# Norm factors in a PSUM bank, a root one step sooner, and two sums finished ahead of a branch, in a two-block kernel

## What is computed

```python
def dsa_attention(q, k, v, q_idx, k_idx, w_idx, rel_bias):
    ...
        p = jax.nn.softmax(logits, axis=-1).astype(v.dtype)
        return jnp.einsum('bqhk,bqkhd->bqhd', p, v_sel)

def hgrn2(q, f_pre, i, g_out, lb, norm_g):
    lb = lb.reshape(B_HEADS, B_HEAD_DIM).astype(jnp.float32)
    f = lb + (1.0 - lb) * jax.nn.sigmoid(f_pre.astype(jnp.float32))
    log_f = jnp.log(f)
    kk = 1.0 - f
    ...
    o = jnp.transpose(o, (1, 0, 3, 2, 4)).reshape(bsz, seq, B_HEADS, B_HEAD_DIM)
    o = rmsnorm_2(o, norm_g) * jax.nn.silu(g_out.astype(jnp.float32))

def hier_moe(h, rg_w, rg_b, re_w, re_b, w_gate, w_up, w_down):
    ...
    for gi in range(N_GROUPS):
        hg = jax.nn.silu(jnp.einsum('nd,edf->nef', x, wg[gi])) * jnp.einsum('nd,edf->nef', x, wu[gi])
        y = y + jnp.einsum('nef,efd->nd', hg * gates[:, gi, :, None], wd[gi])

def second_block(...):
    lb_soft = jax.nn.softmax(hgrn_lb_raw.astype(jnp.float32), axis=0)
    lb_all = jnp.cumsum(lb_soft, axis=0) - lb_soft[0:1]
    ...
    return rmsnorm_2(x, final_norm_g)
```

## Time and profile before

| | us |
|---|---|
| runs, median (lowest to highest) | 2004.6 (2003.86 to 2004.92) |
| the profiled execution, its own time | 2007.65 |
| its span, first to last instruction | 2005.9 |
| PE busy in the span | 1664.8 |
| DVE busy | 985.1 |
| ACT busy | 551.2 |
| POOL busy | 610.1 |
| mean granted clock of PE | 0.936 |

### The profile page before, as it was taken

The page is one execution under the profiler, slowest core; times in us unless marked ns, Lnnn a source line. Parts: engine busy times, 40 slices in busy tenths (PEclk is TensorE's granted clock), DMA queues, the critical chain, the costliest instruction groups (busy, mean ns, idle before and its releaser), DMA issues.

```text
span 2005.9 us, 22036 instructions
## 1 busy us (share of the span) xinstructions
PE 1664.8 (83%) x8692; PEld 1026.3 (51%) x8692; DVE 985.1 (49%) x1895; ACT 551.2 (27%) x959; POOL 610.1 (30%) x396
## 2 busy tenths in 40 slices
PE   7899986777777777778999998999999967677765
PEld 7785842232222223237989988987895311111211
DVE  6462766876778775553573896554434100000001
ACT  4342421212212212114443545445621000000001
POOL 3331633444445444435563205433320000000000
PEclk9999988999999999999999999999999877778778
DMA  8755599999999999995544433544588999999997
GB/s 336 303 196 218 204 366 413 421 421 421 422 421 422 421 421 418 421 380 171 168 147 141 144 126 126 185 168 147 178 349 309 421 421 421 422 421 421 422 421 306
DMA packets 92373, 634.88 MB, mean 317 GB/s; under 512 B 10956, under 2 KB 13772, under 8 KB 16616
## 3 DMA queue, kind: packets, MB, share of 16 engines
q1 hardware_dynamic: 50832, 353.39, 45.2%
q0 software_dynamic: 36864, 268.45, 32.5%
q10 hardware_dynamic: 4568, 11.56, 1.6%
HBM read 632.28 MB, written 1.08 MB: 316 GB/s over the span
## 4 chain that ended last, share of the span: by engine, by line
PE 44%; DMA 39%; DVE 11%; ACT 3%; issue 2%; POOL 0%; ACTq 0%; SPq 0%; DVEq 0%; POOLq 0%
DMA t<-in_expert_uv,t 19%; DMA t<-in_ed 7%; DMA t<-in_eg 6%; PE ps L589 5%; PE ps L594 5%; PE ps L591 5%; DMA ring<-in_ed 4%; PE ps L819 3%; PE ps L653 3%; DVE t L2106 3%; PE ps L822 3%; DMA ring<-in_eg 3%; PE ps L666 3%; PE ps L609 2%; PE ps L610 2%; PE ps L615 2%
## 5 line engine op out<-in xcount | busy, mean ns | idle before, releaser
L181 POOL TENSOR_TENSOR t<-ring,t 128x1024 fp32r<-128x1024 f32 x125 | 315.9, 2540 | 486.8 <-ACT t L173 486.6
L819 PE MATMUL ps<-t 128*128 128x512 f32 x488 | 268.6, 633 | 158.3 <-ACT t L1469 158.1
L2778 POOL DMA_INDIRECT t<-in_expert_uv,t x244 | 275.7, 1130 | 354.8 <-PE ps L822 334.1
L2106 DVE CUSTOM_DVE_ANT_0 t<-t 128x1024 f32<-128x1024 f32 x244 | 299.8, 1234 | 164.4 <-DMA t<-in_expert_uv,t 161.8
L173 ACT ACTIVATE t<-ring 128x1024 fp32r<-128x1024 f32 x220 | 230.1, 1054 | 227.8 <-PE ps L594 77.8
L822 PE MATMUL ps<-t 128*128 128x512 f32 x488 | 254.6, 604 | 0.0
L819 PEld LDWEIGHTS ps<-t 128*128 128x128 f32 x488 | 85.1, 193 | 317.1 <-ACT t L1469 254.5
L1125 PE MATMUL ps<-t 128*32 128x512 f32 x856 | 142.3, 763 | 70.2 <-DMA t<-in_eg 27.7
L181 DVE TENSOR_TENSOR t<-ring,t 128x1024 fp32r<-128x1024 f32 x95 | 131.9, 1395 | 135.0 <-ACT t L173 134.4
L589 PE MATMUL ps<-t 128*128 128x256 f32 x1120 | 165.0, 291 | 12.6 <-ACT t L173 6.6
L1462 ACT ACTIVATE t<-t 128x2 f32<-128x2 f32 x129 | 26.2, 203 | 507.4 <-DVE t L2106 507.0
(11 more groups left out here) (383 smaller groups left out, 1915.4 us busy)
## 6 DMA issues: line engine op xcount, KB each, us to landing
ring<-in_w_in SPq DMA_DIRECT2D x82, 1024.0 KB, 5.0
t<-in_eg SPq DMA_DIRECT2D x43, 1024.0 KB, 26.7
t<-in_ed SPq DMA_DIRECT2D x36, 1024.0 KB, 27.1
t<-in_eu SPq DMA_DIRECT2D x28, 1024.0 KB, 27.0
ring<-in_eu SPq DMA_DIRECT2D x27, 1024.0 KB, 26.4
ring<-in_ed SPq DMA_DIRECT2D x21, 1024.0 KB, 27.0
ring<-in_ada_w SPq DMA_DIRECT2D x20, 1024.0 KB, 7.6
ring<-in_eg SPq DMA_DIRECT2D x17, 1024.0 KB, 27.7
```

What stands on the lines that cost most here:

```text
L181: e.tensor_tensor(p.lo, p.view, p.hi.bitcast(F32), ALU.subtract).then_inc(self.w.lo[eng], 1)
L819: ins = e.matmul(sums[tt][0], s.diag[col % 4], v[:, 1024:1536], start=first, stop=last)
L2106: ins = e.tensor_tensor_reduce(out=g[:, 0:1024], in0=g[:, 0:1024], in1=s.hN[:, col // 128, :], scale=1.0, scalar=0.0, op0=ALU.mult, op1=AL ...
L2778: m.gathered[s.place[col]].up(e.indirect_dma_start(out=s.gb[col], out_offset=None, in_=m.a_in["expert_uv"], in_offset=bass.IndirectOffsetO ...
```

## The change

It has six edits.

- `dve_attention`: the four bound operations stand behind the output subtractions.
- `pe_recurrence`: the bank that would be claimed next is taken out of the ring during the stage, and its first 80 columns are `h.stat`. `dve_recurrence` keeps the sums and the inverse roots there (indices 0 and 3); mean squares, roots and the polishing's temporary stay in SBUF.
- `act_recurrence`: `pour(filler, 2)` for `pour(filler, 4)` ahead of the root.
- `dve_inv_sqrt`, with more than one column: one operation fewer and two fused ones.
- `act_squares`: the first halves are squared ahead of the branch on ACT, the second halves behind it.
- `dve_experts`: the first halves are multiplied with the norm's row ahead of the last result `y(7, 1)`; behind the branch the second halves of both tiles are made by one fused operation each. Both engines' dense paths repeat the early work.

```diff
@@ pe_recurrence
+    whole, kept = list(b.usable), b.usable[b.next % 8]
+    b.usable, b.next = [i for i in b.usable if i != kept], b.next % 8
+    h.stat, h.stat_free = b.ps[kept][:, 0:80], (b.out[kept], b.uses[kept])
...
     pe_turn(m, e, "obT", r3(h.bq, 2), 8, m.h_out)
+    b.usable, b.next = whole, whole.index(kept)
@@ act_recurrence
-    pour(filler, 4)
+    pour(filler, 2)
@@ new, and called ahead of the branch with n = 0 and behind it with n = 1
+def act_squares(m, e, n):
+    o, b = m.s4, m.b
+    junk = o.xg[1].rearrange("p a b -> p (a b)")[:, 0:512]
+    for tt in range(2):
+        e.wait_ge(*b.full(("sum4", tt, n)))
+        ins = e.activation(junk, b.ap(("sum4", tt, n)), ACT.Square, accum_out=o.fin[:, 2 * n + tt:2 * n + tt + 1])
+        if tt == 0:
+            m.a(ins)
+        else:
+            m.norm_sum.up(ins)
+    e.wait_ge(m.norm_sum.sem, m.norm_sum.n)
@@ dve_inv_sqrt
     else:
-        m.v(e.tensor_tensor(t, r, r, ALU.mult))
-        m.v(e.tensor_tensor(t, t, ms, ALU.mult))
-    m.v(e.tensor_scalar(t, t, -0.5, 1.5, ALU.mult, ALU.add))
-    m.v(e.tensor_tensor(r, r, t, ALU.mult))
+        m.v(e.scalar_tensor_tensor(out=t, in0=ms, scalar=-0.5, in1=r, op0=ALU.mult, op1=ALU.mult))
+        m.v(e.tensor_tensor(t, t, r, ALU.mult))
+        m.v(e.scalar_tensor_tensor(out=r, in0=t, scalar=1.5, in1=r, op0=ALU.add, op1=ALU.mult))
@@ dve_recurrence
-    h_ss, h_ms, h_sq, h_r, h_t = (h.sst[:, 16 * i:16 * i + 16] for i in range(5))
+    h_ss, h_ms, h_sq, h_r, h_t = ((h.stat, h.sst)[i in (1, 2, 4)][:, 16 * i:16 * i + 16] for i in range(5))
+    e.wait_ge(*h.stat_free)
@@ dve_experts, ahead of the wait for ("y", q, n)
+            if q == 7 and n:
+                e.wait_ge(m.d_row0.sem, 48)
+                e.wait_ge(*m.norm_sum.turn("dve"))
+                for tt in range(2):
+                    ins = e.tensor_tensor(o.ys[:, tt, :], b.ap(("sum4", tt, 0)), m.grow[0][:, 0:512], ALU.mult)
+                m.v(ins)
@@ vector_program, behind the branch: the same two removed here, and
-    e.wait_ge(*m.norm_sum.turn("dve"))
-    m.v(e.tensor_tensor(hold[:, 0, 512:1024], b.ap(("sum4", 0, 1)), m.grow[0][:, 512:1024], ALU.mult))
...
-    m.fin_row.up(e.tensor_scalar(hold[:, 0, 512:1024], hold[:, 0, 512:1024], f[:, 8:9], None, ALU.mult))
-    m.fin_row.up(e.scalar_tensor_tensor(out=hold[:, 1, 512:1024], in0=b.ap(("sum4", 1, 1)), scalar=f[:, 9:10],
-                                        in1=m.grow[0][:, 512:1024], op0=ALU.mult, op1=ALU.mult))
+    for tt in range(2):
+        m.fin_row.up(e.scalar_tensor_tensor(out=hold[:, tt, 512:1024], in0=b.ap(("sum4", tt, 1)), scalar=f[:, 8 + tt:9 + tt],
+                                            in1=m.grow[0][:, 512:1024], op0=ALU.mult, op1=ALU.mult))
```

More of the change, by code:

```diff
@@ L1785, in act_dense @@
     e.wait_ge(*b.full("sum5"))
+    for tt in range(2):
+        junk = o.xg[1].rearrange("p a b -> p (a b)")[:, tt * 512:tt * 512 + 512]
+        b.emptied(e.activation(junk, b.ap(("sum4", tt, 0)), ACT.Square, accum_out=o.fin[:, tt:tt + 1]), ("sum4", tt, 0))
+    for tt in range(2):
+        e.wait_ge(*b.taken(("sum4", tt, 0)))
+def act_squares(m, e, n):
[9 more added lines that the diff above has]
+    e.wait_ge(m.norm_sum.sem, m.norm_sum.n)
 def scalar_program(m, e):
@@ L1806, in scalar_program @@
     e.activation(m.st[:, 60:61], m.one, ACT.Sqrt)
-    for n in range(2):
-        for tt in range(2):
-            e.wait_ge(*b.full(("sum4", tt, n)))
-            ins = e.activation(o.xg[1].rearrange("p a b -> p (a b)")[:, 0:512], b.ap(("sum4", tt, n)), ACT.Square,
-                               accum_out=o.fin[:, 2 * n + tt:2 * n + tt + 1])
-            if n == 0 and tt == 0:
-                m.a(ins)
-            else:
-                m.norm_sum.up(ins)
-                e.wait_ge(m.norm_sum.sem, m.norm_sum.n)
+    act_squares(m, e, 1)
     e.wait_ge(*m.norm_ms.turn("act"))
@@ L2713, in dve_dense @@
     e.wait_ge(*b.full("sum5"))
+    for tt in range(2):
+        e.wait_ge(*b.taken(("sum4", tt, 0)))
+        m.v(e.tensor_tensor(o.ys[:, tt, :], b.ap(("sum4", tt, 0)), m.grow[0][:, 0:512], ALU.mult))
 def vector_program(m, e):
@@ L2735, in vector_program @@
     hold = r3(m.hold, 2)
-    e.wait_ge(m.d_row0.sem, 48)
-    e.wait_ge(*m.norm_sum.turn("dve"))
-    for tt in range(2):
-        ins = e.tensor_tensor(o.ys[:, tt, :], b.ap(("sum4", tt, 0)), m.grow[0][:, 0:512], ALU.mult)
-    m.v(ins)
-    e.wait_ge(*m.norm_sum.turn("dve"))
-    m.v(e.tensor_tensor(hold[:, 0, 512:1024], b.ap(("sum4", 0, 1)), m.grow[0][:, 512:1024], ALU.mult))
     e.wait_ge(*m.norm_sum.turn("dve"))
```

13 lines of the change are left out of this document (8 added, 5 removed).

## The result

The changed kernel took 1994.11 us (median of five runs, 1992.75 to 1996.77) against 2004.6 for the kernel before: ratio 0.9948, 95% interval 0.9937 to 0.9959. That is 10.5 us less, where 8.8 were forecast. A second series gave 1996.3 against 2004.34, ratio 0.9959 (0.9946 to 0.9973), 8.0 us less. The kernel before in that series ran from 2003.03 to 2008.54, so single runs scatter by several microseconds. A difference of one or two can be read only inside a trace, between two rows.

A forecast was written before the change was run, and what follows sets the result against it. Expert weight streaming fills the DMA engines, so only time saved on TensorE ahead of line 1107 or behind the last weight counts. 4.1 + 2.6 + 0.1 + 1.95 = 8.75 us, giving 1995.8 us; range 1992.8 to 2000.0.

The forecast's parts named there:

- Part 1: Attention's end: moving the four bound operations behind the attention output cuts TensorE's stall; gain 4.1 us, bounds 2.6 and 5.0.
- GpSimd got in first: Attention's end: GpSimd goes ahead of the first low half, leaving TensorE idle 0.87 us instead of 3.45.
- Part 2: Recurrence's norm: sooner root, factors partly in PSUM and one operation fewer bring the transposes together; gain 2.6 us.
- so I keep the slow clock in: Recurrence's norm: a 1.5 us gap stays, so the slow clock behind it is assumed to remain; otherwise gain 4.2.
- even if every operation stayed blocked, 1239.9: Recurrence's norm: with operations blocked as before, products still end at 1239.9, ahead of TensorE's transposes at 1241.69.
- The bank costs nothing: Level loop, seven banks: nearest claim has 2.3 us left, so no cost; slower rival, 2009.9 us, chance 0.04.
- Part 3: Shorter polishing at the end of retrieval, hidden in retention: one operation less; gain 0.1 us (0 to 0.2).
- Part 4: Kernel's end: early squares and products let the sum of squares start 2.05 us sooner; net gain 1.95 us.
- the 3 from which it would have counted: ScalarE's branch at the end: from 3 us each microsecond counts; at 5, time 1997.8; rival's chance 0.08.
- From line 1107 on all rows should be sooner by the same 6.8 us: Routing onward: sign that all rows, and the last weight too, come 6.8 us sooner.
- the 3.05 us between the profiled execution and the median: Whole kernel: the profiled execution lies 3.05 us above the runs' median, turning a 1997.1 span into 1995.8.

The follow-up runs named there:

- experiment 4: The kernel before with only the root of the recurrence's norm taken after two pours instead of four, no bank, old polishing; 2003.79 us, ratio 0.9997.
- experiment 3: The kernel before with the end's edits alone (first halves squared and scaled ahead of the branch), old polishing; 2003.49 us, ratio 0.9992.

## Why the prediction was right, point by point

The time forecast, 1995.8, lies between the two series (1994.11 and 1996.3), and the sum of 8.75 us between their gains. Term by term it was less exact, and that the total fits so well is in part luck.

| place, fourteen traces | values |
|---|---|
| attention, to line 923 | 21.26 to 21.30 (5 with the bounds ahead), 19.39 (two ahead), 17.07 to 17.10 (6 with all four behind), 16.07 and 16.08 (low half first) |
| norm gap | 6.0 to 6.6 (6 without the bank), 3.85 or 3.86 (8 with it) |
| norm stretch | 310.55 to 312.33 (6 without), 307.00 to 307.23 (8 with) |
| end | 8.28 to 8.47 (4 of the old form), 6.33 to 6.84 (9 of the new), 6.09 (short branch) |
| the loop's last step | 7.16 or 7.17 (5), 8.60 to 8.80 (9) |
| routing to groups | 6.72 to 7.06 (8), 8.62 to 8.66 (6) |
| groups to last y product | 447.11 to 447.34 (5), 447.75, 448.29, 449.07 to 449.59 (5), 454.91 and 456.30 (spare matmuls) |

- **Part 1, forecast 4.1, measured 4.2.** Right in size and in mechanism: GpSimd got in first, one turn was lost (idle 0.74, forecast 0.87), the clock held. The four operations in their new place took 0.2 us each.
- **Part 2, forecast 2.6 (4.2 if the slow clock went too), measured 3.9 to 4.4** (310.98, or 311.53 on the mean of the six without the bank, less 307.11). The direct share was 2.3, close to the forecast 2.6. The failing step is the sentence "so I keep the slow clock in": the clock behind the shorter gap stayed up in all eight traces, and that is worth another 1.5 to 1.9 us. The prediction had the row that pointed to it, 384 matmuls at full clock behind 1.50 us of idle time, used it for part 1, and then chose the other side for a gap of the same kind. I also credited the sooner root with half of the work. It had no effect; the cause is that the 16-column operations and the products, kept in SBUF, waited their turn against GpSimd. How much of it is the small operations and how much the two products no run separates. The bound "even if every operation stayed blocked, 1239.9" was refuted by experiment 4: on that scale they were out at about 1244.3, the old time, because a chain that starts sooner meets more of GpSimd's operations.
- **The bank costs nothing: right.** The stretch with the level loop was 146.2 us with seven banks and with eight.
- **Part 3, forecast 0.1.** Not visible where it was put (the traces start attention's end 0.35 us later, within the scatter). At the kernel's end four operations took 0.79 us instead of five in 0.99.
- **Part 4, forecast 1.95, measured 2.0.** VectorE's early products ended at 1984.05, right at the last one, which began at 1984.11. The squares now run while VectorE stands at its branch, but the branch still ended last, as forecast: the sum of squares began 0.35 us behind ScalarE's last sum, where it was 0.11 with the short branch. ScalarE's branch took 1.24 us, well short of the 3 from which it would have counted.
- **"From line 1107 on all rows should be sooner by the same 6.8 us": wrong.** The lead was 9.4 us at routing's start, 11.3 at the groups' first product, 8.9 at the last y product. The first difference was in the profile of the kernel before: it holds three falls of the clock, 1.45, 1.6 and 1.9 us (output columns, the loop's last step, routing), that other traces don't have at the same places, and the changed kernel's trace shares only the 1.6. I took the 3.05 us between the profiled execution and the median as a bare offset and didn't ask where they were spent. The second is the stream's end. The last weights landed at 1981.09 instead of 1991.79, so 10.7 us sooner, not 6.8; but the last y product began 3.76 us behind them instead of 1.92. Of the 2.42 us lost, 1.84 are therefore TensorE's, and 0.6 the stream's. 1.9 to 2.4 us were lost in five of the six traces that have at least two of the bounds moved, the end's edits and no spare matmuls; the sixth, with the late root, lost 0.6. The kernel before and the four with parts of the change lost nothing, the one with the short branch 1.1. In all seven of these that lost, and in none of the five that didn't, the four matmuls of the first half's product ran at the lower level of the clock for all or part of their time, 2.81 to 3.78 us instead of 1.98. Why the clock was down there in these traces and not in the others is **open**. It is not the end's edits by themselves (experiment 3), and the short branch shows that it can happen without any of them.
- **The sum of the parts.** 4.2 + 3.9 + 2.0 + 0.1 = 10.2 us belongs to the code that was changed; less the 2 us at the stream's end it is about 8.2, and the falls that come in one execution and not in the next may, by my estimate from their 1.5 to 1.9 us, move a series by some 2 us to either side. Measured were 10.5 and 8.0. That the total was right is luck to this extent: the clock term left out (1.5) and the loss not foreseen (2) nearly cancel.

## What to carry to other kernels

While GpSimd works in SBUF, price a tiny VectorE operation with all operands in SBUF by GpSimd's running operation, not by its columns. Starting such a chain sooner gave nothing here; moving one operand to PSUM gave nearly all. Price a TensorE gap with the clock behind it, and look in the traces for what the clock did behind a gap like the one that is left. Before a trace is taken as the base of a sum, look for stretches in it where the clock was low without a gap of its own: another execution may not have them.

## What the runs showed of the hardware

- VectorE and GpSimd took turns, one operation each. A VectorE operation of 8 or 16 columns from SBUF to SBUF lasted 1.90 to 2.34 us beside GpSimd's 128x1024 subtractions (line 2404, 0.94), and 0.17 or 0.18 once GpSimd was still or one operand was in PSUM. The reciprocals were an exception: they took 0.19 to 0.25 us in SBUF too, right beside GpSimd. I had expected it of operations with two SBUF inputs alone; the one with a single input (line 1836 in experiment 4) took 2.33 as well. The Trainium skill ("SBUF — State Buffer", section "SBUF: two separate sides") gives both kinds: two SBUF inputs, or one of VectorE's two-port performance modes. The trace agrees that such an operation waits for a whole one of GpSimd's; which mode line 1836 ran in no row shows. The rows add that the wait passes to the next such operation: in the changed kernel line 2420 fell from 0.94 to 0.17 us, and the 2048-column product behind it, line 2421, rose from 2.28 to 2.98.
- At attention's end the clock held behind 3.05 us of idle time (one trace) and fell behind 3.42 to 3.47 us (five of five). The length of the last gap alone does not tell: at the stream's end it fell behind 1.34 us of idle time in the changed kernel and held behind 1.32 in the kernel before.
- The same code at the same place ran at either level from one execution to the next: the loop's last step took 7.16 or 7.17 us in five traces (clock 1.00) and 8.60 to 8.80 in nine (0.81 or 0.82 where I looked).
- A branch over the unused path cost VectorE 2.7 us more than one over nothing, and in all thirteen traces of it an instruction packet ended within 0.5 us of VectorE's going on. ScalarE's cost 0.64 us in one order of work and 1.24 in another, and 0.35 over nothing.
